# PEER experts of a two-layer diffusion step: half of U's products in three rounded passes, 15 row products moved forward

## The reference

```
def peer_ffn(h, w_q, sub_k1, sub_k2, u_tab, v_tab):
    ...
    idx = jnp.take_along_axis(cand_i, pos, axis=-1)
    g = jax.nn.softmax(top_s, axis=-1).astype(h.dtype)
    def chunk(args):
        xc, ic, gc = args
        u = jnp.take(u_tab, ic, axis=0)
        act = jax.nn.gelu(jnp.einsum('chkd,cd->chk', u, xc), approximate=False)
        return jnp.einsum('chk,chkd->cd', gc * act, jnp.take(v_tab, ic, axis=0))
```

## Time and profile before

| | |
|---|---|
| three runs, median (lowest to highest) | 2661.08 us (2657.42 to 2661.69) |
| profiled execution, its own time | 2662.42 us |
| its span in the profile | 2660.6 us |
| TensorE busy | 2502.0 us of the span |
| VectorE, GpSimd, ScalarE busy | 1559.0, 890.6, 507.0 us |
| DMA | 679.46 MB, mean 255 GB/s |

### The profile page before, as it was taken

One profiled execution on the slowest core, in us unless ns is written; L12 is line 12 of the kernel. 1 busy time (PEld: TensorE's weight loads), 2 busy tenths in 40 slices (PEclk: granted clock), 3 DMA queues, 4 the chain that ended last, 5 costly groups with the idle time before them and its releaser, 6 DMA issues.

```text
span 2660.6 us, 30288 instructions
## 1 busy us (share of the span) xinstructions
PE 2502.0 (94%) x11270; PEld 1776.3 (67%) x11270; DVE 1559.0 (59%) x3250; ACT 507.0 (19%) x1060; POOL 890.6 (33%) x650
## 2 busy tenths in 40 slices
PE   5988899999999999999978788999999999999995
PEld 4756699889444566666656567988964446666663
DVE  1345479967455554655445447896755555456654
ACT  2344432133000000000043344212310000000001
POOL 3400360000444544555353215200024445355551
PEclk8999999999999999999989798999999999999997
DMA  6455334654999998999835612365479999899992
GB/s 257 136 190 190 121 111 137 190 147 139 377 388 394 381 383 304 367 389 379 309 122 153 182 41 82 105 191 167 141 271 385 389 382 387 302 376 382 389 374 106
DMA packets 219889, 679.46 MB, mean 255 GB/s; under 512 B 32385, under 2 KB 63153, under 8 KB 219233
## 3 DMA queue, kind: packets, MB, share of 16 engines
q1 hardware_dynamic: 142912, 396.42, 43.8%
q0 software_dynamic: 76832, 281.11, 27.7%
HBM read 658.87 MB, written 18.56 MB: 255 GB/s over the span
## 4 chain that ended last, share of the span: by engine, by line
PE 89%; DVE 3%; DMA 3%; ACT 3%; issue 1%; SPq 1%; POOL 1%; ACTq 0%; DVEq 0%
PE ps L943 33%; PE ps L954 32%; PE ps L657 4%; PE ps L658 4%; PE ps L659 4%; PE ps L932 2%; PE ps L839 2%; PE ps L820 2%; DMA arena<-gelu_half 1%; PE ps L688 1%; PE ps L680 1%; PE ps L829 1%; PE ps L907 1%; DMA arena<-in_w_mod 1%; DMA ring<-in_w_mod 1%
## 5 line engine op out<-in xcount | busy, mean ns | idle before, releaser
L943 PE MATMUL ps<-arena,ring 128*128 128x256 f32 x4096 | 916.7, 380 | 0.0
L954 PE MATMUL ps<-ring,arena 128*128 128x512 f32 x2048 | 901.4, 592 | 1.4 <-DVE arena L1803 1.3
L943 PEld LDWEIGHTS ps<-arena,ring 128*128 128x128 f32 x4096 | 774.2, 190 | 156.7 <-issue 60.3
L954 PEld LDWEIGHTS ps<-ring,arena 128*128 128x128 f32 x2048 | 388.5, 190 | 441.1 <-issue 434.5
L576 POOL DMA_INDIRECT arena<-in_u_rows,arena x256 | 296.4, 1158 | 867.8 <-PE ps L932 534.0
L1803 DVE SCALAR_TENSOR_TENSOR arena<-arena 128x256 f32<-128x256 f32 x256 | 108.7, 425 | 570.4 <-ACT arena L1169 367.2
L576 POOL DMA_INDIRECT arena<-in_v,arena x256 | 335.3, 1310 | 311.7 <-DVE arena L1826 202.2
L1169 ACT ACTIVATE arena<-ps 128x256 f32<-128x256 f32 x256 | 98.3, 384 | 1601.5 <-PE ps L943 1432.1
L536 POOL TENSOR_TENSOR ring_lo<-ring,ring_hi 128x1024 fp32r<-128x1024 f32 x84 | 216.8, 2592 | 427.3 <-ACT ring_hi L1054 427.3
L1826 DVE SCALAR_TENSOR_TENSOR arena<-arena 128x1024 f32<-128x1024 f32 x254 | 325.6, 1282 | 23.3 <-DMA arena<-in_v,arena 5.8
L1812 DVE CUSTOM_DVE_ANT_0 arena<-arena 128x1024 f32<-128x1024 f32 x256 | 305.5, 1221 | 13.5 <-DMA arena<-in_u_rows,arena 13.3
(11 more groups left out here) (213 smaller groups left out, 2133.8 us busy)
## 6 DMA issues: line engine op xcount, KB each, us to landing
ring<-in_u SPq DMA_DIRECT2D x256, 512.0 KB
ring<-in_v SPq DMA_DIRECT2D x256, 512.0 KB
ring<-in_w_mod SPq DMA_DIRECT2D x80, 512.0 KB
ring<-in_w_in SPq DMA_DIRECT2D x36, 512.0 KB
ring<-in_w_q SPq DMA_DIRECT2D x32, 512.0 KB
gelu_half<-arena SPq DMA_DIRECT2D x120, 128.0 KB, 3.8
arena<-gelu_half SPq DMA_DIRECT2D x120, 128.0 KB
arena<-in_w_mod SPq DMA_DIRECT2D x16, 512.0 KB, 18.6
```

The source lines that it names most:

```text
L943: ins = mm(ps[:, 6 + b % 2, 0:STOK], slot[c % RING][:, P * k:P * k + P], HFS[:, k, :], start=(k == 0), stop=(k == KC - 1))
L954: ins = mm(ps[:, t + 3 * q, :], GL[:, b % GLS, P * t - P:P * t], slot[c % RING][:, 512 * q:512 * q + 512], start=(b == MIDDLE[0]), stop=(b ...
```

## The change

U's blocks 64 to 127 are no longer multiplied as plain float32. ScalarE writes the rounded half of a block into one of three places (`high_u`), VectorE subtracts it from the ring's slot to make the low half and frees the slot (`low_u`), and TensorE makes 24 matmuls of 256 columns from the halves in the place of 8 plain ones. The tokens are split once per layer (`xs_hi`, `low_x`). All copies lie where finished blocks of G were. Besides, 15 row products stand between the one-hots, on the two row buffers that are free then, and 72, not 84, in the V half, so 41 are left for the paired blocks; the row sums begin two blocks earlier.

```diff
-EARLY_DOTS = 0
-MIDDLE_DOTS = 84
+EARLY_DOTS = 15
+MIDDLE_DOTS = 72
...
                     c = u_chunk(l, b)
+                    if b >= SPILL:
+                        if b == SPILL:
+                            pe.wait_ge(sem("xs_lo"), l + 1)
+                        pe.wait_ge(used(c % RING), turn_of(c))
+                        for k in range(KC):
+                            r = slice(P * k, P * k + P)
+                            ins = parts(ps[:, 6 + b % 2, 0:STOK], (u_half(b, 0)[:, r], u_half(b, 1)[:, r]),
+                                        (xs_hi[:, k, :], xs_lo[:, k, :]), k == 0, k == KC - 1)
+                        ins.then_inc(sem("us_spent"), 1)
+                        return
                     wait_loaded(pe, c)
...
+                def high_u(b):
+
+                    if b < SPILL + USLOTS:
+                        products_done(min((Q_US - Q_G + 2 * D * (b - SPILL + 1) - 1) // STOK, MIDDLE[-1]))
+                    else:
+                        act.wait_ge(sem("us_spent"), since("us_spent", l) + b - SPILL - USLOTS + 1)
+                    wait_loaded(act, u_chunk(l, b))
+                    fn(u_half(b, 0), slot[u_chunk(l, b) % RING], ACT.Copy).then_inc(sem("us_hi"), 1)
+
+                products_done((Q_US - Q_G - 1) // STOK)
+                fn(xs_hi, HFS, ACT.Copy).then_inc(sem("xs_hi"), 1)
+                high_u(SPILL)
+                high_u(SPILL + 1)
                 for b in range(SPILL, KEYS):
                     if b == SPILL:
                         gelu(b)
+                    if b + 2 < KEYS:
+                        high_u(b + 2)
                     if b + 1 < KEYS:
                         gelu(b + 1)
...
+                def low_x():
+
+                    dve.wait_ge(sem("xs_hi"), l + 1)
+                    tt(xs_lo, HFS, f32(xs_hi), ALU.subtract).then_inc(sem("xs_lo"), 1)
+
+                def low_u(b):
+
+                    c = u_chunk(l, b)
+                    dve.wait_ge(sem("us_hi"), since("us_hi", l) + b - SPILL + 1)
+                    tt(u_half(b, 1), slot[c % RING], f32(u_half(b, 0)), ALU.subtract).then_inc(used(c % RING), 1)
...
                     one_hots(p)
+                    if dots < EARLY_DOTS * p // (PIECES - 1):
+                        dot(dots)
+                        dots += 1
...
+                    if i == SPILL - 10:
+                        low_x()
+                    if i == SPILL - 2:
+                        low_u(SPILL)
+                low_u(SPILL + 1)
                 for b in range(SPILL, KEYS):
                     product(b)
+                    if b + 2 < KEYS:
+                        low_u(b + 2)
...
-                    while b >= SPILL + 18 and sums < P and 44 * sums < P * (b - SPILL - 17):
+                    while b >= SPILL + 16 and sums < P and 44 * sums < P * (b - SPILL - 15):
                         accumulate(sums)
                         sums += 1
```

More of the change, by code:

```diff
@@ L129 @@
 Q_LN, Q_GT, Q_DIAG, Q_WORK = Q_G, Q_G + 2 * D, Q_G + 4 * D, Q_G + 5 * D
+Q_XS = Q_WORK + D
+Q_US = Q_XS + 2 * KC * STOK
+USLOTS = 3
+assert Q_US + USLOTS * 2 * D <= Q_G + SPILL * STOK
 SIGNALS = {
@@ L144 @@
     **dict.fromkeys(("gelu", "w_ready"), [128, 128]),
+    **dict.fromkeys(("us_hi", "us_spent"), [KEYS - SPILL, KEYS - SPILL]),
     **dict.fromkeys(("row_used",), [256, 256]),
@@ L192, in build @@
                       enumerate(("x_hi", "x_lo")))
+        xs, us = in_slab("xs_split", Q_XS, 2 * KC * STOK), in_slab("u_split", Q_US, USLOTS * 2 * D)
         const = sb("const", C_N)
@@ L226, in build, with u_half @@
         HFP = ar(Q_HFP, KC * P).rearrange("p (k t) -> p k t", k=KC)
+        xs_hi, xs_lo = (xs[:, KC * STOK * i:KC * STOK * i + KC * STOK].rearrange("p (k t) -> p k t", k=KC) for i in range(2))
+        def u_half(b, i):
+            at = 2 * D * ((b - SPILL) % USLOTS) + D * i
+            return us[:, at:at + D]
         def modulated(n, k, kn, t):
@@ L1161, in gelu @@
                 def gelu(b):
-                    c = u_chunk(l, b)
-                    act.wait_ge(used(c % RING), turn_of(c))
+                    if b < SPILL:
+                        c = u_chunk(l, b)
+                        act.wait_ge(used(c % RING), turn_of(c))
+                    else:
+                        act.wait_ge(sem("us_spent"), since("us_spent", l) + b - SPILL + 1)
                     if GLS <= b < SPILL:
@@ L1198, in experts, with products_done @@
                             part(p)
+                def products_done(e):
+                    act.wait_ge(sem("w_ready"), since("w_ready", l) + MIDDLE.index(e) + 1)
+                def high_u(b):
+                    if b < SPILL + USLOTS:
+                        products_done(min((Q_US - Q_G + 2 * D * (b - SPILL + 1) - 1) // STOK, MIDDLE[-1]))
+                    else:
+                        act.wait_ge(sem("us_spent"), since("us_spent", l) + b - SPILL - USLOTS + 1)
[5 more added lines that the diff above has]
+                high_u(SPILL + 1)
                 for b in range(SPILL, KEYS):
@@ L1201, in experts @@
                         gelu(b)
+                    if b + 2 < KEYS:
+                        high_u(b + 2)
                     if b + 1 < KEYS:
                         gelu(b + 1)
-                    if b == SPILL + 16:
+                    if b == SPILL + 15:
                         act.wait_ge(sem("p_dots"), l + 1)
@@ L1851, in experts @@
                                 dve.tensor_copy(ss[:, 25:26], HSEL[:, P - 1:P]).then_inc(sem("p_dots"), 1)
-                    if b == SPILL + 18:
+                    if b == SPILL + 16:
                         weigh()
-                    while b >= SPILL + 18 and sums < P and 44 * sums < P * (b - SPILL - 17):
+                    while b >= SPILL + 16 and sums < P and 44 * sums < P * (b - SPILL - 15):
                         accumulate(sums)
```

## The result

The changed kernel takes 2617.6 us (median of 4 runs, 2614.03 to 2623.26) against 2661.28 of the kernel before: a ratio of 0.9841, interval 0.982 to 0.9862, so 1.6% faster. The profiled execution (2623.26 us, span 2621.4) is the longest of the four.

The account below looks back on a forecast made before the run. TensorE alone set the paired blocks before; after the change DMA at 390 GB/s would bind. 2 x 22.9 + 1.3 - 2 x 1 = 45 us off 2662.4 gives 2617, less 1.3 for the median: 2616, range 2593 to 2645.

Parts of the forecast that it names:

- the forecast's own case: Paired blocks: DMA near 390 GB/s, load-to-product chain just hidden; 2616 us, range 2600 to 2638, chance 0.63.
- TensorE's term: Paired blocks: 2.88 + 3.44 + 0.06 us for change of kind, 6.38 a pair, 0.50 less than 6.88.
- DMA's term: Paired blocks: at 390 GB/s kept up, the stage takes 417.4 us against 440.3, 22.9 less per layer.
- The chain: Paired blocks: U's landing, high half, low half, three rows, product and outer make three pairs last at least L + 10.0.
- L: Paired blocks: time for a U load to land after issue; may be 9.4 us at 6.48 a pair, taken as less.
- the slower rival: Paired blocks: gathers slow the ring's loads, L 11.3 us, 7.1 a pair, 22 us more, 2683; chance 0.08.
- the rival named as a small gain: Paired blocks: at L = 10.2 the chain makes 6.73 a pair, gaining 21 us, 2640; chance 0.11.
- The signs: Paired blocks: split step 0.12 us, TensorE idle 5 to 10 us per layer, DMA at 385 to 400 GB/s in row-sum pairs.
- The row products among the one-hots: Among the one-hots: 15 products, 18.3 us, fit into VectorE's waits of 24.5 us; cost 0.
- The V half: V half: demand falls from 388 to 359 GB/s; layer 1's idle 1.3 us goes, nothing else.
- The seam: Start of the pairs: first U block ready at 10.5 us, needed at 10.3; 1 us per layer, bounds 0 and 3.
- the faster rival: Paired blocks: TensorE stays the only bound, DMA gives 411 GB/s or more; 65 us gained, 2596; chance 0.15.

Follow-up runs that it names:

- experiment 6: Changed kernel with 112 row products in the V half in place of 72, 1 left for the pairs: 2667.8 us, ratio 1.0043.
- 2: Changed kernel with U's block b + 3 loaded before V's block b + 1 in the pairs: 2584.54 us, ratio 0.9711.
- experiment 10: Changed kernel with one additional 1.06 us copy on ScalarE ahead of each high half: 2645.36 us, ratio 0.9935.
- 3: Kernel before with only the row products moved and row sums two blocks earlier, U still plain float32: 2656.51 us, ratio 0.9994.
- 8: Changed kernel with U loaded ahead of V and the row products back where they were: 2586.03 us, ratio 0.9732.
- 4: Changed kernel with the row products back where they were, U's blocks still split: 2622.32 us, ratio 0.9863.
- 11: Changed kernel with U loaded ahead of V and one additional ScalarE copy ahead of each high half: 2583.68 us, ratio 0.9723.

## Why the prediction was right, and where its reasons were not

The time was right: 2616 predicted, 2617.6 measured, in the range of the forecast's own case. (The 45 us forecast are 44 by the medians and 39 by the two profiled executions.) The working holds in part, and that the sum came out right is luck.

- **TensorE's term** held. A split product steps at 0.12 us. The 0.06 us for a change of kind is 0: a pair lasts 6.30 us where nothing else binds. So TensorE alone would have given 0.57 a pair, 73 us in all, not 64.
- **DMA's term failed as a cause.** "I take 390 as what can be kept up" was read from stages that asked for 388 GB/s or less at TensorE's pace (layer 1's waited 1.2 us in all), so they couldn't show more. Asked for more, DMA gave 402 (experiment 6), and 402 to 408 in row-sum pairs where TensorE was hardly idle (2). At 402 the pairs with 2.62 MB would take 6.5 us at worst, and those with row sums would be TensorE's; with U ahead of V even the first kind step at 6.31. The parts of the sum are off in opposite ways: it gave the first 14 pairs, with the most bytes, 6.72 us, and the 44 with row sums 6.48. Measured in layer 0 and 1, V products step at 6.48 and 6.56 us in the first 14, and at 6.65 and 6.71 in the row-sum pairs. The DMA share gave no warning: it reads 1.00 at 379 GB/s and 1.03 at 408.
- **The chain took its place.** The prediction had it as "U lands L later", L + 10.0 for three pairs, weighed L between 3 and 10.2 us and took "less than 9.4". L is no single number: from U's issue to its high half it is 8.6 us in the median and 9.9 and 10.5 at most in the two layers. A late block stops TensorE (L is 10.0 in the chain above, so 20 us for three pairs), and an early one gives nothing back. So the steps average 6.58 us in layer 0 and 6.65 in layer 1 ahead of the last four pairs, between the forecast's 6.48 and 6.72. The argument that L falls back because "gathers thin out as soon as VectorE is late" is borne out by little: in experiment 10, where VectorE is later, DMA moves 371 GB/s and the median falls from 8.7 to 8.5 us in the row-sum pairs of layer 0. What keeps L off the 11.3 of the slower rival was not tested. So two causes had nearly the same price here, and the sum came out right by that; the rival named as a small gain was the mechanism, at the price of the forecast.
- **The signs** named beforehand could not tell the two causes apart: DMA at 385 to 400 GB/s came true (392 and 389), and TensorE's idle time in the pairs was 10.8 and 14.6 us a layer instead of 5 to 10.
- **Two sums** don't follow from their terms. A ring at half of 390 would move 1.05 MB in 5.4 us, and with the 3.2 us taken for issue and completion L would be 8.6, not "about 7". And 407 GB/s with no loss at the seam gives 2597, not 2600.
- **The row products among the one-hots** cost 0, as said: the stretch is 256.1 us before and after. They gave nothing measurable either (3 and 8), and with the change's own order at most some 5 us, unsettled (4).
- **The V half** held: layer 1's idle 1.2 us is gone, layer 0 is nearly as before (idle for 0.6 us).
- **The seam** was put at 1 us per layer. The first four V products of each layer's pairs follow each other at 6.31 us, and the fifth is the first to wait (925.87 in the chain above), for a later U block; no cost of the seam itself is seen.
- **Low and high half** took 1.23 and 1.06 us, as the rows of other lines had it; VectorE, busy for 65% of the span, and GpSimd, for 35%, had time to spare; what counted was the place of VectorE's instructions in the chain.

The 425 GB/s of the Trainium skill (DMA: Bandwidth & Descriptors, Bandwidth) was not reached by a stage here: the highest rate over 260 us is 408. The 411 of the faster rival was not reached over that time either, and it wasn't needed. At 6.31 us a pair, the 111.1 MB of the 44 row-sum pairs are 400 GB/s, which experiments 2 and 11 moved. The rival failed because the chain stood in the way, not for want of bandwidth.

## What to carry to other kernels

A rate of a stage is a capacity only if somebody in it asked for more, and a busy share of 1.00 doesn't say that; before calling DMA the bound, find a stage that starves or make one, and check that it starves for bytes. When work is inserted between a load and its use (here two halves on two engines), write the chain from the event that issues the load to the event that next frees a slot, divide by the number of tiles it spans, and look at what is queued ahead of each link. Put a spread into it where a landing time goes, as late blocks cost and early ones give nothing back. One load moved ahead of another won 33 us (1.3%), one instruction moved behind three won 26, and both kept every byte and every matmul. A cheap test tells latency from capacity: put a microsecond on an engine with time to spare and see if the kernel gets longer.

## What the runs showed of the hardware

- An indirect DMA to 64 of 128 partitions isn't half the price: with 0.26 MB gathers in the place of 0.52 MB the DMA engines stood at a share of 1.00 with 255 GB/s, where gathers over 128 partitions went with 392 GB/s at 1.01. By columns instead (a plain DMA of 512 of 1024, from neighbouring rows) the same bytes left the share at 0.81, with 283 GB/s. Why the half set of partitions is slow was not tried further.
- A mix of 0.52 MB loads and 128-partition gathers reached 402 to 408 GB/s over stretches of 220 to 260 us, at a share of 1.01 to 1.03 (experiments 2, 6 and 11).
- A 0.52 MB load of U, issued 0.37 us behind one of V while nine gathers were issued between 902 and 917 us, landed 9.6 us after its issue; 8.6 us is the median from U's issue to the start of its high half in the changed kernel.
- TensorE passed between plain float32 and float32r products, twice in 6.31 us, with no measurable gap.
